# Attention over eight pairs of heads: the order of every engine is drawn up from a table of durations, and the projections are spread over all pairs

## The reference, cut to what matters

```
proj = _rmsnorm(x, b_norm_pre[j]) @ b_w_in[j]
q, z = jnp.split(proj, 2, axis=-1)
...
z = jnp.einsum('bqhd,bkhd->bhqk', q, k, preferred_element_type=jnp.float32) * scale
causal = kpos[None, :] < qpos[:, None]
log_keep = jnp.where(causal, jax.nn.log_sigmoid(-z), 0.0)
rev = lax.cumsum(log_keep, axis=log_keep.ndim - 1, reverse=True)
...
a = jnp.exp(log_a)
o = jnp.einsum('bhqk,bkhd->bqhd', a, v.astype(jnp.float32))
...
h = (jax.nn.silu(z) * o.reshape(b, T, D_ATTN)) @ b_w_out[j]
```

## Time and profile before

| | us |
|---|---|
| median of 3 runs (2906.8 to 2909.09) | 2907.31 |
| the profiled execution, time | 2905.56 |
| the profiled execution, span | 2904.0 |
| PE busy over the span | 2828.8 (97%) |
| DVE, ACT, POOL busy | 1646.3, 1343.3, 1157.7 |

### The profile page before, as it was taken

One profiled execution on the slowest core, in us unless ns is written; L12 is line 12 of the kernel. 1 busy time (PEld: TensorE's weight loads), 2 busy tenths in 40 slices (PEclk: granted clock), 3 DMA queues, 4 the chain that ended last, 5 costly groups with the idle time before them and its releaser, 6 DMA issues. The chain is left out here.

```text
span 2904.0 us, 42069 instructions
## 1 busy us (share of the span) xinstructions
PE 2828.8 (97%) x14856; PEld 2460.1 (85%) x14856; DVE 1646.3 (57%) x2150; ACT 1343.3 (46%) x2746; POOL 1157.7 (40%) x1023
## 2 busy tenths in 40 slices
PE   7999999999999999999989999999999999989998
PEld 6999999999978788889978888888888888867886
DVE  5322132212344431012278888888888899888775
ACT  6010000000143420111278788878888888875542
POOL 3233233323120110012276767676767676752010
PEclk9999999999999999999999999999999999999999
DMA  5111111111154354435586767767676777957773
GB/s 159 33 27 35 42 37 29 30 37 37 66 166 132 111 184 166 149 108 161 178 242 205 228 210 225 213 217 221 209 229 200 231 217 230 290 175 215 234 224 110
DMA packets 286311, 451.16 MB, mean 155 GB/s; under 512 B 52898, under 2 KB 223010, under 8 KB 280132
## 3 DMA queue, kind: packets, MB, share of 16 engines
q1 hardware_dynamic: 275108, 409.23, 45.7%
q0 software_dynamic: 11040, 39.86, 4.6%
HBM read 325.22 MB, written 123.81 MB: 155 GB/s over the span
## 5 line engine op out<-in xcount | busy, mean ns | idle before, releaser
L1739 POOL TENSOR_TENSOR a_a<-a_a,a_prod 128x512 f32<-128x512 f32 (+3 forms) x640 | 664.3, 1048 | 368.9 <-DVE a_prod L1689 254.9
L1689 DVE TENSOR_TENSOR_SCAN a_prod<-a_keep,a_prod,a_restart 128x513 f32<-128x513 f32 x384 | 488.6, 1273 | 0.2 <-ACT a_keep L1630 0.2
L1699 DVE TENSOR_TENSOR a_atl<-a_pt,a_ath 128x512 fp32r<-128x512 f32 (+3 forms) x640 | 377.8, 598 | 116.7 <-ACT a_ath L1639 111.7
L1629 ACT ACTIVATE a_a<-a_pz 128x512 f32<-128x512 f32 (+3 forms) x640 | 350.9, 548 | 125.1 <-PE a_pz L1551 112.7
L1639 ACT ACTIVATE a_ath<-a_pt 128x512 fp32r<-128x512 f32 (+3 forms) x640 | 347.5, 554 | 90.3 <-PE a_pt L1576 87.4
L1630 ACT ACTIVATE a_keep<-a_pz 128x512 f32<-128x512 f32 (+3 forms) x640 | 354.6, 554 | 0.0
L1576 PE MATMUL a_pt<-ident,a_a 128*128 128x128 f32 x2176 | 340.9, 273 | 5.6 <-POOL a_a L1739 2.7
L1576 PEld LDWEIGHTS a_pt<-ident,a_a 128*128 128x128 f32 x2176 | 271.5, 140 | 60.9 <-DVE a_atl L1699 5.0
L1561 PE MATMUL a_po<-a_ath,a_v 128*128 128x512 f32 (+3 forms) x640 | 281.8, 440 | 13.4 <-DVE a_atl L1699 7.3
L277 POOL TENSOR_TENSOR w_wh<-w_raw,w_gain 128x1024 fp32r<-128x1024 f32 x22 | 41.7, 1895 | 535.1 <-PE v_pg L347 279.9
L1550 PE MATMUL a_pz<-a_kh,a_q 128*128 128x512 f32 (+3 forms) x640 | 240.4, 379 | 10.5 <-ACT a_keep L1630 8.3
(11 more groups left out here) (233 smaller groups left out, 6173.8 us busy)
## 6 DMA issues: line engine op xcount, KB each, us to landing
a_x<-x_d SPq DMA_DIRECT2D x96, 896.0 KB, 5.8
a_x<-x_d SPq DMA_DIRECT2D x64, 832.0 KB, 5.5
a_kh<-kh_t SPq DMA_DIRECT2D x32, 512.0 KB, 11.1
a_kl<-kl_t SPq DMA_DIRECT2D x32, 512.0 KB, 14.4
w_raw<-in_a_w_in POOLq DMA_DIRECT2D x30, 512.0 KB, 4.8
x<-f_xn POOLq DMA_DIRECT2D x17, 512.0 KB, 5.2
g_y_in<-sz_t SPq DMA_DIRECT2D x17, 512.0 KB, 7.6
g_x<-x SPq DMA_DIRECT2D x17, 512.0 KB, 3.7
```

The source lines that it names most:

```text
L1629: act.activation(a[:, s, q, 0:w], pz[:, n % ZS, 0:w], ACT.Sigmoid, scale=SCALE)
L1689: dve.tensor_tensor_scan(prod[:, s, 0:w + 1][:, ::-1], keep[:, n % KS, 0:w + 1][:, ::-1], restart[:, 0:1].broadcast_to([P, w + 1]), prod[: ...
L1699: dve.tensor_tensor(atl[:, b % AS, c0:], pt[:, turn_slot(hh, b), c0:], ath[:, b % AS, c0:].bitcast(F32), ALU.subtract).then_inc(at_split, 1)
L1739: pool.tensor_tensor(part, part, prod[:, n % PS, after:after + w], ALU.mult).then_inc(weighted, 1)
```

## The change

The due times go. While the program is built, `Line` plays the phase through with a table of durations: at each step every engine offers the next item of each kind (`heads`) with the time at which what it needs is there; the item that can start first is placed, ties going by `RANK`. Buffers count as needs: transposes need the low part three blocks back, a high part needs the product four back. Chunks form one list of 280 over all eight pairs (pair 7's last ones end at 96% of the attention work), and a chunk is offered once it is no more than six chunks early. What comes out is one fixed list for each engine, SP's too. In code: PE's `value` is parted in `turn` and `product` items, each with its place; a head's values are split by POOL where the list says so, behind a wait for the last product of the head two before; SP loads keys and queries in separate steps.

```diff
-LEAD = 4300
-BEHIND = {"PE": 0, "ACT": 150, "DVE": 600, "POOL": 200, "SP": 1000}
-GATE_BEHIND = {"PE": 0, "ACT": 250, "DVE": 250, "POOL": 0, "SP": 1500}
-ZS, TS, US, KS, PS, AS, LAG = 2, 3, 4, 4, 8, 4, 2
+ZS, TS, US, KS, PS, AS = 2, 3, 4, 4, 8, 4
...
-def chunks(pr):
...
-def schedule(pr, who):
...
+SCORE_LEAD, CHUNKS_END, CHUNKS_FROM, CHUNK_PACE = 13, 0.96, -0.01, 6
+def pe_time(w):
+    return w / 2400 + 0.0155
+def act_time(w):
+    return 0.050 + 0.000833 * w
+def dve_time(w):
+    return 0.048 + 0.00104 * w
+def pool_time(w):
+    return 0.09 + 0.00224 * w
...
+class Line:
...
+    def heads(self, engine):
+        i = self.next
+        if engine == "PE":
+            if i["score"] < len(self.pieces):
+                k = i["score"]
+                h, n = self.pieces[k]
+                needs = [self.back("sigmoid", k, ZS)] + ([("keys", h)] if n == 0 else [])
...
+            if i["turn"] < len(self.blocks):
+                k = i["turn"]
+                h, b = self.blocks[k]
+                u, j = BLOCKS[b]
+                needs = [self.back("low", k, TS)]
+                if j == 0:
+                    needs.append(("weigh", h * N_PIECE + QG * u + QG - 1))
+                yield "turn", self.when(*needs), RANK["turn"]
+            if i["product"] < i["turn"]:
+                k = i["product"]
+                h, b = self.blocks[k]
+                needs = [("low", k)]
+                if begins_group(b):
+                    needs.append(self.back("out", i["out group"], 1))
+                if b == 0:
+                    needs.append(("values", h))
+                yield "product", self.when(*needs), RANK["product"]
+            if i["chunk"] < len(self.chunks):
+                k = i["chunk"]
+                pr, gx, m, part = self.chunks[k]
+                needs = [("x", pr, gx, part)]
+                if part == 0:
+                    needs.append(self.back("gated", k // PARTS, 1))
+                if gx == 0 and part % (PARTS // 2) == 0:
+                    needs.append(("split", pr, m, part // (PARTS // 2)))
+                due = CHUNKS_FROM + (CHUNKS_END - CHUNKS_FROM) * k / len(self.chunks)
+                behind = self.spent / self.whole - due
+                step = 1 / len(self.chunks)
+                if behind > -CHUNK_PACE * step or i["turn"] == len(self.blocks):
+                    yield "chunk", self.when(*needs), RANK["chunk due"] if behind > 0 else RANK["chunk"]
...
+            if i["high"] < len(self.blocks):
+                k = i["high"]
+                yield "high", self.when(("turn", k), self.back("product", k, AS)), RANK["high"]
...
+            if i["scan"] < len(self.pieces):
+                k = i["scan"]
+                yield "scan", self.when(("sigmoid", k), self.back("weigh", k, PS)), RANK["scan"]
+            if i["low"] < len(self.blocks):
+                yield "low", self.when(("high", i["low"])), RANK["low"]
...
+            if i["weigh"] < len(self.pieces):
+                yield "weigh", self.when(("scan", i["weigh"])), RANK["weigh"]
+            if i["values"] < N_HEAD:
+                h = i["values"]
+                yield "values", self.when(("v_in", h), self.back("product", (h + 1) * N_BLOCK - 1, 2 * N_BLOCK)), RANK["values"]
+            if i["split"] < len(self.splits):
+                pr, m, half = self.splits[i["split"]]
+                yield "split", self.when(("raw", pr, m), ("used", pr - 1, m) if pr else ("used", None)), RANK["split"]
...
+        took, seen = self.work_of(what, k)
+        self.free[engine] = end = start + took
...
+    def draw_up(self):
+        while True:
+            best = None
+            for e in ENGINES:
+                for what, ready, rank in self.heads(e):
+                    if ready is not None:
+                        start = max(self.free[e], ready)
+                        key = start, ENGINES.index(e), rank
+                        if best is None or key < best[0]:
+                            best = key, e, what, start
+            if best is None:
+                break
+            self.place(*best[1:])
...
+        self.lines["SP"] = [x[1:] for x in sorted(self.lines["SP"], key=lambda x: x[0])]
...
+X_LANDS, V_LANDS, LANDS = (5.0, 16.0, 17.0, 18.0), 10.0, 8.0
+RANK = {"score soon": 0, "product": 2.7, "chunk due": 1.5, "turn": 2, "score": 3, "chunk": 4, "out": 0, "high": 1, "open": 2,
+        "sigmoid": 3, "low": 2.7, "gated": 2, "scan": 3, "values": 2.7, "weigh": 1, "split": 2}
...
-                        if not is_pair(pr, 0):
-                            sp.wait_ge(q_stored, 32 * NGX * pr)
-                            apart(sp, passed_sp)
-                        load(pr + 1, hh)
+                        load(pr + 1, hh, keys)
...
+                elif what == "queries" and not last:
+                    if not is_pair(pr, 0):
+                        sp.wait_ge(q_stored, 32 * NGX * pr)
+                        apart(sp, passed_sp)
+                    load(pr + 1, hh, queries)
...
-            def value(pr, hh, b):
+            def turn(pr, hh, b):
-                if b == LAG:
-                    pe.wait_ge(v_ready[hh], pr + 1)
                 if j == 0:
                     pe.wait_ge(weighted, piece(pr, hh, QG * u + QG) + N_PIECE)
-                before = turn_before(pr, hh, b)
-                if before:
-                    pe.wait_ge(at_split, blk(*before) + 1)
+                wait_past(pe, at_split, blk(pr, hh, b) + 1 - TS)
...
-                for lag in (LAG + 1, LAG):
-                    before = lagged(pr, hh, b, lag)
-                    if before and begins_group(before[2]) == (lag > LAG):
-                        multiply(*before)
...
-                if is_pair(pr, 0) and hh == 0 and n == QG:
-                    split_v(0, 0)
...
+                if not is_pair(pr, 0):
+                    apart(pool, passed)
+                    pool.wait_ge(av_done, blk(pr, hh, 0))
...
-            def value(pr, hh, b):
-                if b == N_BLOCK // 2:
-                    if hh == 0:
-                        pool.wait_ge(av_done, blk(pr, 0, 0) + N_BLOCK)
-                        split_v(pr, 1)
-                    elif not is_pair(pr, NPAIR - 1):
-                        pool.wait_ge(av_done, blk(pr, 1, 0) + N_BLOCK)
-                        split_v(pr + 1, 0)
```

315 lines of the change are left out of this document (214 added, 101 removed).

## The result

The changed kernel takes 2923.17 us (median of 5 runs, 2920.23 to 2927.2) against 2906.8 of the kernel before on the same chip (2905.38 to 2909.09): ratio 1.0056, 95% interval 1.0041 to 1.007. It is 16 us slower. The forecast was 2871, in a range of 2848 to 2898 and with a chance of 0.10 on slower; it was wrong by 52 us.

What follows compares the result with a forecast made beforehand. PE was taken to bound the kernel, DVE holding it back in pairs 6 and 7. Waits of 32 us instead of 66.6 (less 34.6), clock less 1.5, next phase plus 1: 2905.56 became 2870.5, forecast 2871, range 2848 to 2898.

Steps and rivals of the forecast that it cites:

- Loads: Key, query and value loads on SP's queue, issued in new places: come in time and cost nothing.
- The clock: PE's granted clock over the phase: one drop less, 1.5 us gained.
- PE without a wait, 1075.9 us: PE's scores, products, transposes and chunks in the phase: 1075.9 us of work, unchanged by the change.
- The order by needs: Planned order, mostly pairs 1 to 6: waits at the middle's rate would be 30.6 us; 18 taken as left.
- The even pace: Chunks moved from pairs 1 to 5 into pairs 6 and 7: the end's separate 29.9 us of waits go.
- The start: First part of the phase, PE's turns behind POOL's value splits: waits 12 us, before 12.5.
- The end of the phase: Last chunk's store, next phase's loads and last scores: next phase 1 us longer, drain stays at 2 us.
- Rival C: DVE becomes the bound across the phase; at its middle share of 88.5%, 2916 us, slower; chance 0.07.
- Rival D: POOL's value split stops PE once in each of 16 heads, also costing clock: 67 us more, 2938 us; chance 0.04.
- Rival B: Only the balance over pairs pays, the middle's wait rate stays: 21.5 us less waits, 2885 us; chance 0.22.
- Rival A: Nearly all PE waits go, leaving 8 us start, 5 middle, 2 end: 2852.5 us; chance 0.19.
- The signs: If right: pairs 1 to 6 about 139 us, DVE over 90% busy, low-part waits under 10 us, copy waits nearly gone.

Runs made afterwards that it cites:

- the two kernels with the old pace: Kernel before with only SyncE's loads moved (2902.62 us), and the newly planned orders with values early, loads behind the gate's store, chunks even within each pair (2881.2 us).
- the best version: Changed kernel with mended start, values one gap sooner, six key and query loads per gap, pair 7's second head's split over two gaps: 2869.24 us, 0.9875.

## Why the prediction was wrong, point by point

- **The step that failed is "Loads".** It said "Cost nothing", and it looked only at whether the moved loads themselves come in time (keys before their scores, values before their split). They do. It did not ask what is queued behind them: the x loads, whose due time is the shortest of all. Ten waits of 14.1, 2.7, 5.1, 4.2, 3.1, 5.1, 1.0, 2.3, 5.5 and 4.2 us make 47 us (from start to start, less a matmul's own time; 49.7 on the weight loads). I had the answer in hand: the earlier trace rows show a load landing after 23.8 us behind others on this queue, and I used it for POOL only. Shown by taking the loads out (2880), by moving them in the kernel before (2989), by moving them to the gap with the values ahead (2873.6), and by letting them write all partitions (2871.3). With that last edit the step as forecast is nearly true, and the time is the forecast's 2871. That the two are the same number is in part luck: a wait of 6.0 us for x is left at the start, and the order and the pace, below, were off in opposite directions.
- **The clock** was put at 1.5 us better. In the phase 27.3 us of full speed are missing (8 + 17 + 3 by the three stretches, whose clocks are rounded to 0.01), where the forecast left 6.3. But 9.6 of them fell while PE stood in a wait and cost nothing beyond it. What the clock cost by itself is 17.7 us (before 4.9), 11.4 more than forecast.
- **The account:** 1174.7 us of phase less 1075.9 of work are 98.8. Forecast were 45: 32 of waits, 6.3 of clock, 6.7 of rest. Measured: 79.0 of waits of the weight loads (49.7 for x, 29.3 for all else), 17.7 of clock outside of them, 2.1 of rest. So 47.0 + 11.4 - 4.6 = 54 us over the 1121. Without x the orders left 29.3 us of waits, about what was said; the queue, and the clock behind its waits, lost the rest.
- **PE without a wait, 1075.9 us:** held, since only 2.1 us are left unexplained. The best version's phase is 1119.7 us, forecast 1121.
- **The order by needs** was right, and more than that: 21.4 us between the two kernels with the old pace, where the forecast gave it 13 (30.6 less 18). One reading in it was off: 6.7 + 6.5 of 24.2 us is 55%, not two thirds.
- **The even pace** was right in kind and two to four times too large: 5.9 to 12 us, where the forecast had 21.5 for the balance alone. The finer order with the old pace has already taken most of the low part's waits out of the end: 5.5 + 2.2 us in pairs 6 and 7, where the earlier trace rows had 18.4. The two terms overlap, and I had priced the pace on the old order.
- **The start:** of the 12 us for waits, 10 came without x (5.9 for sigmoids, 2.2, 1.6 for the low part, 0.7), and the waits that it gave to POOL's value splits did not come. The step looked at POOL's splits and not at SyncE's list, where the fetch stood first.
- **The end of the phase:** held, 293 us behind it.
- **Rival C** (DVE at its share) falls: DVE is busy 788.97 of 846 us, 93.3%, beside a full PE. **Rival D** had the kind right (ten waits of 1.0 to 14.1 us, half-speed clock behind eight of them; it set its edge at nine) and the place wrong: it spoke of POOL's value split. That place did appear, once the loads in the gap pushed the value loads back. **Rival B** is not what happened either, since the order paid. **Rival A** gave the middle 5 us of waits; the best version comes to 8.1 there, but to 36 in the whole phase where A had 15.
- **The signs:** low part under 10 us, right (5.4); copy nearly gone, right (2.7); DVE over 90% busy in pairs 1 to 6, wrong in the changed kernel (84.8 to 92.4%), right in the best version (91.3 to 93.5%); 139 us a pair, wrong in the changed kernel (pair 1 took 152 us), right in the best version (137.6 to 138.7 in pairs 1 to 5, 141 in pair 6); a granted clock under 1.00 in the middle, the sign of D, was there.

## What to carry to other kernels

When a change reorders a queue, price each transfer by what stands ahead of it there, in bytes, and compare the landing with the work that covers it: the transfer that suffers is not the one that moved but the urgent one behind it. Put bulk loads behind the last urgent load of a round, where the round itself leaves a gap, and let small loads that an in-order engine waits for go ahead of the bulk; spreading the bulk between urgent loads was the worst place tried in the changed kernel. Before that, look at GB/s and not at the share of busy DMA engines: loads that write only the lower or only the upper half of the partitions ran at half the rate, and writing every second partition took nine of the ten waits away in three lines. A planner that gives each transfer one landing time sees none of this, and two gains that both take away the same waits must be priced in turn, not each against the old profile.

## What the runs showed of the hardware that was not expected

- Issuing a DMA from SyncE, mostly 0.3 to 0.6 us, took 14.69 us for one (`sz_t`, 224 KB) and 20.07 us for two (`w_raw`, 18.85 of it for the first), with nine and ten DMAs of the queue not yet landed. So the items behind are late twice: SyncE itself stands, and their buffers' states are not looked at meanwhile. The key and query loads are not what it takes: in the kernel before the same store took 7.8 to 9.0 us at six pair starts (8.76 at 1766.22), with nine smaller DMAs not landed and none of those loads among them. The count alone does not tell either, since issues of 0.6 us are found with ten not landed. In all these long ones a value load (`a_v_in`) had just been issued. Which resource fills up was not tried.
- A load that writes the 64 lower or the 64 upper partitions moves at half the rate. The changed kernel with its six loads under way, and behind them; then the version with every second partition, with the six under way:

```profile
1687.00:1700.00 13.00, 12.30 (x66) 10.15 (x65) 12.30 (x17) 11.67 (x26) 8.51 (x8) 1.00 1.02 216
1701.00:1704.00 3.00, 0.00 (x0) 0.00 (x0) 0.79 (x1) 0.00 (x0) 1.26 (x1) 0.58 1.01 410
```

```profile
1671.00:1681.00 10.00, 10.00 (x57) 8.67 (x56) 8.78 (x13) 8.61 (x23) 5.79 (x7) 1.00 0.98 403
```

  216 GB/s against 410 and 403, at a full DMA share in all three: the share says that the queues are busy, not that they are fast. The Trainium skill, DMA: Bandwidth & Descriptors, Where 436 GB/s comes from, gives the rate by 16 ports into the memory, 435 GB/s, and its section The descriptor swizzle puts partitions 0 to 63 on eight of them; by that page half of it, an estimate of 218, is what such a load can reach. The trace agrees with its 216, and 64 partitions spread over the whole width reach the rate of 128: 403 against 410.
- One wait of 5 us was enough to halve TensorE's clock for the next 4 to 5 us (0.37 in place of 0.20 us for a 448 wide matmul). The waits of 1.0 and 2.3 us for x in the changed kernel cost no clock, and the kernel before had 55 waits up to 1.2 us in its middle at a granted clock of 1.00. The Trainium skill, TensorE: Matmul & The Clock Gate, HAM oscillation — how this bites in real kernels, tells of waits for DMAs that slow the clock of the work behind them; the trace agrees, and this, not the micro-idles weighed in the prediction, was the rule that bore on the change.
